# A hybrid mixer with a grouped mixture of experts on one core: first expert's products moved around the tables' product, SyncE waits by pass counts, last norm taken earlier in a pass

## The reference

```python
x = layer_norm(ALPHA * x + merged @ w_out[l], ln1_g[l], ln1_b[l])
moe_out = grouped_moe(x, router_w, router_b, moe_w_gate[l], moe_w_up[l], moe_w_down[l])
x = layer_norm(ALPHA * x + moe_out, ln2_g[l], ln2_b[l])
```

## Time and profile before

| | us |
|---|---|
| median of 3 runs (lowest, highest) | 1067.61 (1065.42, 1068.81) |
| the profiled execution | 1068.2 |
| its span, first to last instruction | 1066.2 |
| PE busy | 977.2 (92%) |
| DVE busy | 474.2 (44%) |
| ACT busy | 293.0 (27%) |
| POOL busy | 226.2 (21%) |

### The profile page before, as it was taken

One profiled execution on the slowest core, in us unless ns is written; L12 is line 12 of the kernel. 1 busy time (PEld: TensorE's weight loads), 2 busy tenths in 40 slices (PEclk: granted clock), 3 DMA queues, 4 the chain that ended last, 5 costly groups with the idle time before them and its releaser, 6 DMA issues.

```text
span 1066.2 us, 17637 instructions
## 1 busy us (share of the span) xinstructions
PE 977.2 (92%) x6604; PEld 432.2 (41%) x6605; DVE 474.2 (44%) x1053; ACT 293.0 (27%) x480; POOL 226.2 (21%) x336
## 2 busy tenths in 40 slices
PE   7999999999999999999997889989888888887774
PEld 3644455455456446444444333333333333332221
DVE  0696464464464464423238333334434444443333
ACT  1114312322223233100034232333333333332221
POOL 3000010010010000033033233333333333333322
PEclk9999999999999999999999999999999999999998
DMA  9432311221211220483937999999999999999992
GB/s 282 127 82 59 80 41 42 59 60 25 67 51 42 60 59 4 158 306 137 394 135 277 382 412 416 380 417 416 414 416 414 416 415 414 415 415 415 416 402 107
DMA packets 96900, 256.68 MB, mean 241 GB/s; under 512 B 17484, under 2 KB 62540, under 8 KB 72016
## 3 DMA queue, kind: packets, MB, share of 16 engines
q1 hardware_dynamic: 85024, 240.57, 59.2%
q0 software_dynamic: 11024, 13.20, 3.6%
q10 hardware_dynamic: 800, 2.15, 0.5%
HBM read 260.66 MB, written 21.23 MB: 264 GB/s over the span
## 4 chain that ended last, share of the span: by engine, by line
PE 53%; DMA 16%; SPq 11%; DVE 8%; issue 7%; POOL 3%; ACT 2%; POOLq 1%; PEld 0%; ACTq 0%; DVEq 0%; PEldq 0%
PE proj L1465 12%; SPq L506 11%; PE proj L1424 11%; DMA y_rows<-const,raw 7%; PE proj L1656 5%; PE bank L1645 5%; PE bank L1567 4%; PE bank L1785 4%; DMA xT_sb<-w_gu 3%; DMA ring<-w_gu 3%; DMA pass_sb<-x_rows,raw 3%; PE bank L1806 2%; PE proj L1432 2%; PE proj L1443 1%; DVE arena L1010 1%
## 5 line engine op out<-in xcount | busy, mean ns | idle before, releaser
L1465 PE MATMUL proj<-xT_sb,ring 128*128 128x512 f32 x384 | 186.3, 611 | 0.0
L1785 PE MATMUL bank<-arena 128*64 128x512 f32 x544 | 122.2, 596 | 17.2 <-PE bank L1806 9.5
L1424 PE MATMUL proj<-xT_sb,ring 128*128 128x512 f32 (+1 forms) x272 | 119.1, 594 | 0.0
L1348 DVE TENSOR_TENSOR const<-bank,const 128x512 f32<-128x512 f32 x33 | 22.8, 691 | 161.6 <-DMA const<-y_rows,raw 161.6
L1465 PEld LDWEIGHTS proj<-xT_sb,ring 128*128 128x128 f32 x384 | 67.0, 189 | 63.0 <-issue 59.2
L1785 PEld LDWEIGHTS bank<-arena 128*64 128x64 f32 x544 | 43.0, 137 | 96.3 <-issue 82.3
L1424 PEld LDWEIGHTS proj<-xT_sb,ring 128*128 128x128 f32 (+1 forms) x272 | 50.8, 188 | 64.6 <-issue 64.5
L853 ACT ACTIVATE pass_sb<-bank 128x256 f32<-128x256 f32 x33 | 12.7, 383 | 196.5 <-PE bank L1785 196.5
L1785 PE MATMUL bank<-gates,arena 128*64 128x512 f32 x256 | 57.4, 596 | 7.8 <-PE bank L1806 4.1
L595 POOL DMA_INDIRECT const<-y_rows,raw x33 | 34.6, 1050 | 125.6 <-DMA y_rows<-const,raw 124.8
L544 POOL MEMSET arena<- 64x64 f32 x8 | 1.2, 145 | 277.1 <-DVE arena L1027 243.3
(11 more groups left out here) (311 smaller groups left out, 1336.5 us busy)
## 6 DMA issues: line engine op xcount, KB each, us to landing
arena<-w_gu SPq DMA_DIRECT2D x64, 1024.0 KB, 22.8
gates<-w_gu SPq DMA_DIRECT2D x32, 1024.0 KB, 22.6
arena<-w_down SPq DMA_DIRECT2D x24, 1024.0 KB, 26.8
ring<-w_in SPq DMA_DIRECT2D x42, 512.0 KB, 3.9
gates<-w_down SPq DMA_DIRECT2D x16, 1024.0 KB, 24.4
xT_sb<-w_gu SPq DMA_DIRECT2D x16, 1024.0 KB, 25.8
branches<-w_down SPq DMA_DIRECT2D x16, 1024.0 KB, 26.5
ring<-w_gu SPq DMA_DIRECT2D x16, 1024.0 KB, 25.0
```

Source lines behind the costliest of these rows:

```text
L1424: ins = pe.matmul(proj[0:w, b, :], ring[:, slot, k, 0:w], xT_sb[:, k, :], start=(k == 0), stop=(k == KT - 1))
L1465: ins = pe.matmul(proj[:, gate_at["bank"], :], ring[:, gate_at["slot"], k, :], xT_sb[:, k, :], start=(k == 0), stop=(k == KT - 1))
L1785: ins = pe.matmul(bank[SLOTS * h:SLOTS * h + SLOTS, 0, :], xeT[:, k % 4, SLOTS * (k // 4):SLOTS * (k // 4) + SLOTS], gu[k // 2][:, k % 2, ...
```

## The change

- **PE, start of the loop.** The first pass is written out: chunks 0 and 1 of expert 0's gate and up, the tables' product, a small product that spreads the last norm's second row, chunks 2 and 3, then the rest of the pass; the next rows are turned at its end. Four `keep_clock` products ahead of the tables' product are gone, and two of five beside the router.
- **PE, every pass.** `pair_stats` stands between chunk 2 and chunk 3 of gate and up. `s_used` is raised six times in every pass. The wait for the end of the pass stands at the end of the pass (`down`), ahead of the `If` and of the next expert's two register reads. Experts 0 to 3 are written out, the loop covers 4 to 31.
- **ACT and DVE.** The last norm of pass p-1 (`normed`, `deviation`) comes ahead of pass p's silu and product; before, it came after them.
- **SP.** `reload` waits for `s_used` to reach six times the expert's last pass, read from a new table `last_i`; the four broadcast loads of the last norm's rows (128 KB each) are gone, one load of 8 KB takes their place early on.
- **Router.** Ranks and the first rows' one-hot product are done for tiles 0 and 1 first, then for 2 and 3; `gates_part(0)` moves behind the second part.

```diff
 # SyncE
+            def home_of_rows(n):
+                sp.wait_ge(s_x1st[n], 32)
+                sp.wait_ge(s_onehot, n + 1)
+                load(3, n, 3)
...
-            sp.wait_ge(s_more, 1)
-            for i, dst in ((0, y_e), (1, x2)):
-                for h in range(2):
-                    at = 2 * SGU + 2 * D + D * i + T * h
-                    sp.dma_start(dst[SLOTS * h:SLOTS * h + SLOTS, :],
-                                 rows[:, at:at + T].partition_broadcast(SLOTS).rearrange("p a d -> p (a d)")).then_inc(s_lnback, 16)
-            def reload(e, b, used):
-                for c in range(NCH):
-                    sp.wait_ge(s_used, used + c + 2)
+            def last_pass(e):
+                return sp.value_load(last_i[0:1, bass.ds(e, 1)], min_val=0, max_val=PASSES - 1)
+            def reload(e, b, last, chunks=range(NCH)):
+                for c in chunks:
+                    sp.wait_ge(s_used, last * NCH + (c + 1))
...
+            sp.wait_ge(s_first, 1)
+            last = last_pass(0)
+            reload(SETS, 0, last, (0,))
+            home_of_rows(1)
+            reload(SETS, 0, last, (1, 2))
             sp.wait_ge(s_tab, 1)
             load(2, 5, 2)
+            reload(SETS, 0, last, (3, 4, 5))
 # ScalarE, one pass
+                if not first:
+                    deviation(p - 1)
                 act.activation(warm[:, 1:2], warm[:, 0:1], ACT.Silu)
...
                 act.wait_ge(s_hp, p + 1)
                 act.activation(h_e, bank[:, 0, 0:FE // 2], ACT.Silu).then_inc(s_silu, 1)
...
-                if not first and n is not None:
-                    deviation(p - 1)
 # VectorE
-            gates_part(0)
+            first_slots(0)
             best_group(2, True)
...
+            first_slots(2)
+            gates_part(0)
             gates_part(2)
...
+            dve.tensor_tensor(last_i[:, :], count[:, INCL, :], C("iota")[:, 0:N_EXP], ADD).then_inc(s_first, 1)
...
                 for n in range(2):
                     p = dve.snap(i * 2 + n, min_val=2, max_val=N_EXP - 1)
+                    normed(p - 1)
                     products(p)
-                    normed(p - 1)
                     finish(p, n)
 # TensorE
+            def down(p, b, loads):
+                pe.wait_ge(s_hT, p + 1)
+                pe.wait_ge(s_ye, p + 1)
...
+                    ins.then_inc(s_yp if c else s_used, 1)
+                pe.wait_ge(s_yp, p + 2)
+                pe.sem_inc(s_used, 1)
+            def one_pass(p, b, loads):
+                pe.wait_ge(s_xeT, p + 1)
+                gate_up(b, loads, (0, 1, 2))
+                pair_stats(p)
+                gate_up(b, loads, (3,))
+                turn(p + 1)
+                h_turned(p)
+                down(p, b, loads)
...
+            def gains(i):
+                for q in range(2):
+                    for h in range(2):
+                        at = 4 * i + 2 * h + q
+                        ins = pe.matmul(proj[SLOTS * h:SLOTS * h + SLOTS, i, T // 2 * q:T // 2 * q + T // 2],
+                                        C("ident")[0:8, at:at + 1].broadcast_to([8, SLOTS]), ln2_in, start=True, stop=True)
+                ins.then_inc(s_gains, 1)
+            turn(0, first=True)
...
+            gains(0)
...
+            gate_up(0, 16, (0, 1))
+            table()
+            gains(1)
+            gate_up(0, 16, (2, 3))
+            pair_stats(0)
+            h_turned(0)
+            down(0, 0, 16)
+            turn(1)
+            pe.wait_ge(s_first, 2)
-            def expert(e, b, loads):
+            def expert(e, b, loads, begun=False):
                 extra = pe.value_load(extra_i[0:1, bass.ds(e, 1)], min_val=0, max_val=MORE)
                 first = pe.value_load(first_i[0:1, bass.ds(e, 1)], min_val=0, max_val=PASSES - 2)
-                pe.wait_ge(s_yp, first + 1)
-                pe.sem_inc(s_used, 1)
+                if not begun:
+                    one_pass(first, b, loads)
                 with pe.If(extra > 0):
                     with pe.Fori(0, extra) as n:
-                        one_pass(first + n, b, loads, False)
-                one_pass(first + extra, b, loads, True)
-            with pe.Fori(0, N_EXP // SETS) as i:
+                        one_pass(first + n + 1, b, loads)
+            for b in range(SETS):
+                expert(b, b, 16, begun=(b == 0))
+            with pe.Fori(1, N_EXP // SETS) as i:
                 for b in range(SETS):
                     expert(pe.snap(i * SETS + b, min_val=0, max_val=N_EXP - 1), b, i * 16 + 16)
```

More of the change, by code:

```diff
@@ L359, in program @@
         count = late("raw", raw_flat, 6 * N_EXP).rearrange("p (i n) -> p i n", i=6)
+        ln2_in = late("raw", raw_flat, T // 2)[0:8, :]
         assert place["raw"] <= 2 * (T + 1)
@@ L1736, in _ @@
             pe.wait_ge(s_chosen, 2)
-            counted(2, False, True).then_inc(s_rank, 1)
+            ranks(range(3, 5), "ones", slice(3, 4), start=False, stop=False)
+            ranks(range(4, 5), "ones", slice(4, 5), start=False, stop=False)
+            ranks(range(2, 4), "earlier", slice(3, 5), start=False, stop=True).then_inc(s_rank, 1)
             pe.wait_ge(s_x1, TT)
-            for c in range(TT):
-                pe.wait_ge(s_firsthot, c + 1)
-                for h in range(2):
-                    ins = pe.matmul(bank[SLOTS * h:SLOTS * h + SLOTS, 0, :], first_hot[:, c, :], x1[:, c, T * h:T * h + T],
-                                    start=(c == 0), stop=(c == TT - 1))
+            for c in (2, 3):
+                ins = first_rows(c)
             ins.then_inc(s_onehot, 1)
@@ L1756, in turn @@
                 ins.then_inc(s_xeTp, 1)
-            turn(0, first=True)
-            for _ in range(4):
-                keep_clock(3 * P)
-            for n in range(TOPK * TT):
-                if n % 2 == 0:
-                    pe.wait_ge(s_hot, n // 2 + 2)
-                if n == 0:
-                    pe.wait_ge(s_copied, 4)
-                for h in range(2):
-                    ins = pe.matmul(bank[SLOTS * h:SLOTS * h + SLOTS, 4, 0:3 * PASSES], slot_hot[:, n, :], pass_hot[:, n, :, :],
-                                    start=(n == 0), stop=(n == TOPK * TT - 1))
-            ins.then_inc(s_tabp, 1)
             def pair_stats(p):
@@ L1796, in one_pass @@
                 ins.then_inc(s_hTp, 1)
-                if last:
-                    pe.sem_inc(s_used, 1)
+                pe.sem_inc(s_used, 1)
+            def down(p, b, loads):
                 pe.wait_ge(s_hT, p + 1)
                 pe.wait_ge(s_ye, p + 1)
-                wd = [v.rearrange("p (f h n) -> p f h n", f=2, h=2) for v in w_chunk[b][4:6]]
-                for f in range(4):
-                    if f % 2 == 0:
-                        pe.wait_ge(s_w[b][4 + f // 2], loads)
-                    for h in range(2):
-                        ins = pe.matmul(bank[SLOTS * h:SLOTS * h + SLOTS, 1, :], hT[:, f % 2, SLOTS * (f // 2):SLOTS * (f // 2) + SLOTS],
-                                        wd[f // 2][:, f % 2, h, :], start=(f == 0), stop=(f == 3))
-                    if f == 1 and last:
-                        ins.then_inc(s_used, 1)
@@ L1810, in one_pass @@
-                ins.then_inc(s_yp, 1)
-            pe.wait_ge(s_first, 1)
-            pe.sem_inc(s_yp, 1)
-            def expert(e, b, loads):
+                for c in range(2):
+                    pe.wait_ge(s_w[b][4 + c], loads)
+                    w = w_chunk[b][4 + c].rearrange("p (f h n) -> p f h n", f=2, h=2)
+                    for f in range(2):
+                        for h in range(2):
+                            ins = pe.matmul(bank[SLOTS * h:SLOTS * h + SLOTS, 1, :], hT[:, f, SLOTS * c:SLOTS * c + SLOTS],
+                                            w[:, f, h, :], start=(c == 0 and f == 0), stop=(c == 1 and f == 1))
+                    ins.then_inc(s_yp if c else s_used, 1)
@@ new lines, in down, with table @@
+                pe.wait_ge(s_yp, p + 2)
+                pe.sem_inc(s_used, 1)
+            def one_pass(p, b, loads):
[4 more added lines that the diff above has]
+                turn(p + 1)
+                h_turned(p)
+                down(p, b, loads)
+            def table():
+                pe.wait_ge(s_copied, 4)
+                for n in range(TOPK * TT):
+                    if n % 2 == 0:
+                        pe.wait_ge(s_hot, n // 2 + 2)
+                    for h in range(2):
+                        ins = pe.matmul(bank[SLOTS * h:SLOTS * h + SLOTS, 4, 0:3 * PASSES], slot_hot[:, n, :], pass_hot[:, n, :, :],
+                                        start=(n == 0), stop=(n == TOPK * TT - 1))
+                ins.then_inc(s_tabp, 1)
```

142 lines of the change are left out of this document (72 added, 70 removed).

## The result

The changed kernel takes 1147.45 us (median of 4 runs, 1143.61 to 1149.06) beside 1067.02 (1065.42 to 1068.81) for the kernel before: 1.074 times as long, interval 1.0731 to 1.0757. Predicted were 1116 and a range of 1070 to 1150. The direction and the wait that makes the loss were right; the size was 31 us short, mainly since the clock was priced too low. The profiled execution took 1147.35 (span 1145.4), with a mean granted clock of 0.958, before 0.991.

A forecast was written before the change was run, and what follows sets the result against it. The DMA weight queue was taken to bound the kernel, PE's chain close behind. A pass of 13.38 + 1.75 + 0.28 + 0.4 = 15.8 us makes PE the bound; 31 passes plus start and end give 1116 us, range 1070 to 1150.

The forecast's parts named there:

- the break-even of 14.3: PE's expert loop: pass time in us above which PE's chain, not the weight queue, sets the end; before, 13.38.
- The rival that the reads stay hidden: PE between passes: register reads not exposed, pass 14.06 us, queue sets the end, 1062.6 us; chance 0.10.
- silu's 0.40: ACT, every pass: silu behind the last norm's root and table load starts 0.4 us later; bounds 0.1 and 0.8.
- with the clock mostly at 2.4 GHz: PE, likeliest case: full read stretch exposed, clock mostly at its upper level, 1116 us; chance 0.57.
- a rival at 0.2: PE's clock falls after the new gap, up to 2.8 us each, in a third of passes: 1144 us; chance 0.2.
- late passes wait 1.28 us for a chunk: PE's late passes before the change: waits up to 1.28 us without a clock fall, cited against the falling clock.
- the 2.67 us of the earlier trace: PE before the change: after this idle time the clock was 0.52 and a down product took 6.42, not 3.65.
- the likeliest case: Full read stretch exposed with the clock mostly at 2.4 GHz: 1116 us, own range 1100 to 1132; chance 0.57.
- the second pass at 600.3: PE's start: written-out first pass, then wait, transposes and reads; second pass about 600.3 against 600.72, bounds 598 and 602.
- the clock products that go cost nothing: PE's start: removing keep_clock products costs nothing, as real products take their place.
- 10.5 was forecast: End: last down product's end to span's end 10.5 us, the last sum's scatter wait going, -1.05.
- I take nothing: PE, pair_stats between chunks 2 and 3: no wait for late statistics is added beyond its row of 0.28 us.

The follow-up runs named there:

- The old order in a pass: Changed kernel with statistics behind gate-and-up and norm behind silu and product again, reads still behind the wait: 1132.75 us, ratio 1.0594.
- the filled gap: Changed kernel with four useless products of 256 columns put behind the wait, between passes on PE: 1107.82 us, ratio 1.0370.
- the half-filled gap: Changed kernel with two useless products of 256 columns behind the wait, leaving part of the idle time: 1107.21 us, ratio 1.0370.
- The run with the early norm in the last pass only: Changed kernel with reads first and old order, but early norm and statistics ahead of chunk 3 in the last expert alone: 1063.05 us, ratio 0.9959.
- the kernel without clock products: Changed kernel with reads first and old order, less the three useless clock products ahead of the ranks of tiles 2 and 3: 1063.37 us, ratio 0.9962.
- the kernel with them: Changed kernel with register reads ahead of the wait and the old order inside a pass, clock products kept: 1063.00 us, again 1063.94.

## Why the prediction was right, and by what it fell short

**Right: the wait.** The step on which all stood, that a wait holds PE's sequencer and whatever stands behind it, is shown both ways: moved back, 81 us go; moved alone, 63 come (1130.38 beside 1067.74 for the kernel before on the same chip). The rival that the reads stay hidden falls with it.

**Right: PE as the bound.** A pass came out above the break-even of 14.3 in every kernel with the moved wait, but for the two-pass expert, which reads once. Without falls it takes 15.30 where 15.8 was forecast: 2.1 to 2.2 of gap for 2.34 (the reads run 1.5, not 1.65), 2.5 to 2.8 where the loop's branch comes, once in four, 0.12 for `pair_stats` in place of 0.28 (its four instructions overlap chunk 3's), silu's 0.40 exactly. The old order in a pass shows the sum of the last two: 31 x 0.52 less the 1.05 at the end is 15.1, measured 14.7.

**Mis-sized: the clock.** The step that failed is "with the clock mostly at 2.4 GHz". A fall was a rival at 0.2, in a third of the passes at 2.8 each. It came in 24 of 32 passes at 1.4 to 1.7, some 39 us; the filled gap shows that these go when PE has work in the gap. The reason given against it, that late passes wait 1.28 us for a chunk without a fall, holds, as the half-filled gap shows; but the row that bore on the new gap was the 2.67 us of the earlier trace rows, and it should have weighed more. The Trainium skill, "TensorE: Matmul & The Clock Gate", A second HAM failure mode, tells of the clock swinging when TensorE idles briefly between groups of products, and says that what is lost is throughput between the bursts. The runs agree as to the swing; but where the Trainium skill has the usual product at its time at full clock, here the products themselves are longer (7.07 for 5.37). The prediction left the rival at 0.2.

**Luck in the range.** 1147 lies in 1070 to 1150, but outside the likeliest case's own 1100 to 1132. The range was drawn to hold falls in up to a third of the passes, 28 us; 39 came. That the time stayed inside is owed to the passes, which without falls were some 11 us shorter in sum than forecast.

**Off by 2.7: the start.** Forecast was the second pass at 600.3; it came at 602.97. What follows the tables' product was right: 10.2 from its end to the first down product's end (588.90 to 599.12) where 10.1 was forecast, then 3.85 to the second pass where it was 4.0. Late was the tables' product itself, which ended at 588.90, not 586.2: 1.17 from ahead of the edit, and 1.51 from DVE's wait for ranks that queue on PE behind the split one-hot product. The prediction counted DVE's steps there, but not PE's queue ahead of them, and that queue is late only at the lower clock. The run with the early norm in the last pass only has the same router, and in its profiled execution the clock stays up (PE, DVE, window):

```profile
567.74 1.94 PE L1744 MATMUL proj<-ring,pass_sb 128*64 128x512 f32 x8 [0.51 <-DVE pass_sb L1261]
574.24 0.55 DVE L1261 TENSOR_SCALAR pass_sb<-const,bank,raw 128x64 f32<-128x64 f32 x2 [0.19 <-PE bank L1738]
568.00:574.00 6.00, 5.25 (x24) 2.37 (x20) 5.31 (x34) 0.90 (x1) 4.69 (x2) 1.00 0.99 358
```

DVE waits 0.19 in place of 1.51 there. What "the clock products that go cost nothing" left out is the price of a low clock in this stretch, now that products which others wait for stand in it. Whether the two that went beside the router would have kept the clock up isn't shown: with all five, the run with the wait moved alone has 0.73 at 568:574 too. It lost nothing by that (its tables' product starts at 584.02, before at 583.76): in the old order that stretch is mostly useless products.

**Right: the end.** 10.5 where 10.5 was forecast.

**The sum again**, with what was measured: 2.7 at the start; 31 passes 516.99 (602.97 to 1119.96) for 490.2, that is 26.8 more, of which 23 falls make 37.6 and the shorter pass -10.8; the last pass 14.91 for 13.4, one more fall; the end 0.0. Together 31.0, the distance from 1116.4 to 1147.35.

**The rival's 1062 was worked out for hidden reads** with the new order; that kernel takes 1066.5. Its pass of 14.06 left out that statistics come late at that pace: 1.88, 0.17, 0.54 and 0.68 us of waits in the third to the sixth pass. With a second pass that starts at 599.56 (reckoned: 598), they hold the two-pass expert's second pass back to 671.37 (reckoned: 667.6). "I take nothing" was right at 15.3 us a pass and wrong at 13.5.

**Still open.** Why some gaps leave the clock up: all eight of 2.5 us or more brought it down, and 16 of the 23 between 2.07 and 2.38; among these 23 the length doesn't tell the two kinds apart.

## What to carry to other kernels

As the runs show for PE, a wait in its program holds its sequencer, so register reads and branches belong ahead of it, where the work that is waited for hides them. Before a wait or an idle time is put between full products in a loop, look in the trace for what the clock did after one of like length, and price a fall in every pass, not in some. A step moved to an earlier place has to be checked at the pace that it is meant to bring: its inputs may be ready in a slow loop and late in a fast one.

## What was not expected of the hardware

- Of 31 idle times of 2.07 to 2.87 us ahead of gate-and-up's 128x512 products, 24 were followed by slow ones; gaps of the same length with 1.1 us of useless products at their front never were. Two useless products were as good as four (1107.2 and 1107.8).
- A fall also comes without so long an idle time. In kernels where gaps between passes are 0.31, single down products took 5.35 for 3.65 behind 2.8 us of waits and small transposes (at 635.54 in the kernel without clock products, waits of 1.06 and 0.53); others behind 2.7 us of the like did not (at 648.42 in the kernel with them, waits of 0.92 and 0.53).
- A branch in PE's sequencer took 208 to 338 ns, and the two register reads with their arithmetic 1.5, whether hidden or not.
